# Weight splits spread over the slots behind the block ends of a merged stage, and shared between two engines around the projections

## The reference, cut to what matters

```python
h = rms_norm(x, norm_g); z = h @ w_in               # q, k, v, gates of both branches
# A: dilated window attention, 3 groups of 8 heads;  B: differential attention, 4 heads
ya = o_a * silu(ga);  yb = rms_norm(o_b, subln_g) * (1 - lam_init) * silu(gb)
pa = ya @ w_proj_a;   pb = yb @ w_proj_b
m = sigmoid(ma) * pa + sigmoid(mb) * pb
return x + m @ w_out                                # and the updated key/value caches
```

## Time and profile before

| | |
|---|---|
| median of 3 runs | 1908.26 us (1905.12 to 1911.16) |
| profiled execution | 1910.81 us, span 1908.8 us |
| mean granted TensorE clock | 0.938 |
| TensorE busy | 1681.4 us (88%) |
| VectorE, ScalarE, GpSimd busy | 707.4, 599.8, 680.1 us |
| chain that ended last, by engine | PE 76%, issue 6%, DMA 5%, POOL 5%, DVE 3%, ACT 2% |

### The profile page before, as it was taken

The page is one execution under the profiler, slowest core; times in us unless marked ns, Lnnn a source line. Parts: engine busy times, 40 slices in busy tenths (PEclk is TensorE's granted clock), DMA queues, the critical chain, the costliest instruction groups (busy, mean ns, idle before and its releaser), DMA issues.

```text
span 1908.8 us, 38064 instructions
## 1 busy us (share of the span) xinstructions
PE 1681.4 (88%) x14552; PEld 1371.5 (72%) x14552; DVE 707.4 (37%) x1751; ACT 599.8 (31%) x1393; POOL 680.1 (36%) x971
## 2 busy tenths in 40 slices
PE   4899698999899998999989779796879878789798
PEld 3677465788799998999977557574657646568587
DVE  4321266322272223622154433343344243358511
ACT  3321265422163222622152332333233233212200
POOL 3654311256443555345472310212121210266420
PEclk8999899999899998999989889798899988889899
DMA  4147400465515565265325757868678676655232
GB/s 150 45 153 266 156 24 21 159 214 186 186 42 197 208 219 186 58 229 193 106 77 186 256 189 241 265 230 283 210 265 259 230 264 230 199 172 195 92 120 83
DMA packets 164252, 336.24 MB, mean 176 GB/s; under 512 B 29873, under 2 KB 50738, under 8 KB 162674
## 3 DMA queue, kind: packets, MB, share of 16 engines
q1 hardware_dynamic: 142514, 212.86, 34.3%
q10 hardware_dynamic: 21568, 121.04, 18.0%
HBM read 294.05 MB, written 127.07 MB: 221 GB/s over the span
## 4 chain that ended last, share of the span: by engine, by line
PE 76%; issue 6%; DMA 5%; POOL 5%; DVE 3%; ACT 2%; SPq 2%; ACTq 0%; DVEq 0%; POOLq 0%
PE ps L1809 16%; PE ps L1810 15%; PE ps L1811 15%; PE ps L2004 4%; PE ps L1948 4%; DMA raw<-in_w_in 3%; PE ps L1899 3%; PE ps L1968 3%; PE ps L2046 3%; POOL w_lo L876 2%; PE ps L1955 2%; PE ps L1807 2%; PE ps L1808 2%; PE ps L2029 2%; PE ps L1920 1%
## 5 line engine op out<-in xcount | busy, mean ns | idle before, releaser
L1809 PE MATMUL ps<-w_hi,hT 128*128 128x512 f32 x1168 | 487.6, 417 | 27.9 <-issue 14.0
L1810 PE MATMUL ps<-w_lo,hT 128*128 128x512 f32 x1168 | 471.8, 404 | 0.0
L1811 PE MATMUL ps<-w_hi,hT 128*128 128x512 f32 x1168 | 471.6, 404 | 0.0
L876 POOL TENSOR_TENSOR w_lo<-raw,w_hi 128x512 fp32r<-128x512 f32 x145 | 185.6, 1288 | 436.0 <-ACT w_hi L1065 435.8
L1809 PEld LDWEIGHTS ps<-w_hi,hT 128*128 128x128 f32 x1168 | 275.1, 236 | 67.3 <-issue 18.3
L1811 PEld LDWEIGHTS ps<-w_hi,hT 128*128 128x128 f32 x1168 | 274.5, 235 | 37.6
L1810 PEld LDWEIGHTS ps<-w_lo,hT 128*128 128x128 f32 x1168 | 275.4, 236 | 33.2
L1546 DVE STREAM_TRANSPOSE k_in<-k_in 128x512 f32<-128x512 f32 x232 | 151.2, 689 | 129.2 <-DMA k_in<-in_cache_b_kv 69.8
L1065 ACT ACTIVATE w_hi<-raw 128x512 fp32r<-128x512 f32 x153 | 95.4, 630 | 266.5 <-DMA raw<-in_w_in 246.9
L969 POOL COPY q_rep<-qTs 32x96 f32<-32x96 f32 (+1 forms) x256 | 59.3, 232 | 212.9 <-issue 115.3
L856 POOL TENSOR_TENSOR rs<-ss,half_pow 128x8 f32<-128x8 f32 (+3 forms) x81 | 127.0, 1568 | 6.7
(11 more groups left out here) (217 smaller groups left out, 2583.7 us busy)
## 6 DMA issues: line engine op xcount, KB each, us to landing
out<-in_cache_a_kv ACTq DMA_DIRECT2D x32, 2040.0 KB, 9.3
k_in<-in_cache_b_kv SPq DMA_DIRECT2D x128, 256.0 KB, 4.0
v_in<-in_cache_b_kv SPq DMA_DIRECT2D x128, 256.0 KB, 4.8
raw<-in_w_in SPq DMA_DIRECT2D x104, 256.0 KB, 4.0
k_in<-in_cache_a_kv SPq DMA_DIRECT2D x104, 256.0 KB, 5.9
v_in<-in_cache_a_kv SPq DMA_DIRECT2D x104, 256.0 KB, 4.3
out<-in_cache_a_kv ACTq DMA_DIRECT2D x8, 2016.0 KB, 9.5
raw<-in_w_in ACTq DMA_DIRECT2D x40, 256.0 KB, 5.7
```

Of the source, the lines that this page charges most:

```text
L876: pool.tensor_tensor(lo, raw[:, q % 4, :], hi.bitcast(F32), ALU.subtract).then_inc(lo_done, 1)
L1809: pe.matmul(z, hi, wh, start=first, stop=False)
L1810: pe.matmul(z, hi, wl, start=False, stop=False)
L1811: return pe.matmul(z, lo, wh, start=False, stop=last)
```

## The change

Four things. (1) The gate table moves: the ninth tiles now stand in slots 6, 18, 30, 42 and 54, always with three slots without gates behind, and the last gates of the table in 58 to 68 in place of 56 to 66. (2) The seven splits at a block end leave `gate`: they stand two, two, two and one in the four slots behind the ninth tile, behind the copies of probabilities and the exponents; the spare chunk is split six slots behind the ninth tile; the raw loads stand behind the copies, one slot after the split of the chunk four before. (3) From chunk 153 to 167 the even chunks' w_lo is VectorE's. The first three splits of block b stand before `move_y(1, 0)`, the first three of the output block before `move_m(7)`. (4) `y_prepare` is cut in two, and tile 1's branch a part goes ahead of GpSimd's later splits; `turn_y(1, 0)` goes from before the last gate to behind `project(0, 0)`.

```diff
-GATE_SLOTS = (*range(7), *range(10, 19), *range(21, 30), *range(33, 42), *range(44, 53), 56, 58, 60, 62, 64, 66)
+GATE_SLOTS = (*range(7), *range(10, 19), *range(22, 31), *range(34, 43), *range(46, 55), 58, 60, 62, 64, 66, 68)
+BLOCK_ENDS = (6, 18, 30, 42, 54)
...
+        def by_vector(q):
+
+            return Q_PA <= q < Q_PB or (Q_PB < q < Q_OUT + KC and q % 2 == 0)
...
+        split_slot = {Q_GATE + KC: 2}
+        for block_, end_ in enumerate(BLOCK_ENDS):
+            q0 = Q_GATE + KC * (block_ + 1)
+            for k in range(1, KC):
+                split_slot[q0 + k] = end_ + (k + 1) // 2
+            if block_ < 4:
+                split_slot[q0 + KC] = end_ + 6
+        load_slot = {q + 4: at_ + 1 for q, at_ in split_slot.items() if q + 4 < Q_PA + 3}
...
         def prefetched(m):
 
-            if m == GATE_TILES - 3:
-                return range(Q_PB, Q_PB + SPARE)
...
+            return range(Q_PB, Q_PB + SPARE) if m == GATE_TILES - 3 else ()
...
+            splits_of(range(Q_PB + SPARE, Q_PB + 4))
+            y_prepare_a(1)
+            splits_of(range(Q_PB + 4, Q_OUT + SPARE))
...
+            def load_raw(q):
+                act.wait_ge(*lo_ready(q - 4))
+                act.dma_start(raw[:, q % 4, :], chunk_source(q)).then_inc(raw_in[q % 4], 16)
...
+                for q in loads_at(gg):
+                    load_raw(q)
...
+                for q in splits_at(gg):
+                    split_hi(*divmod(q, KC))
...
             store_gate(GATE_TILES - 1)
             move_y(0, 0)
+            for q in range(Q_PB + SPARE, Q_PB + 4):
+                split_hi(*divmod(q, KC))
             move_y(1, 0)
-            for q in range(Q_PB + SPARE, Q_OUT + SPARE):
+            for q in range(Q_PB + 4, Q_OUT + SPARE):
                 split_hi(*divmod(q, KC))
...
                 if i + 1 < TILES:
                     move_y(1, i + 1)
+                else:
+                    for q in range(Q_OUT + SPARE, Q_OUT + 4):
+                        split_hi(*divmod(q, KC))
                 if i:
                     move_m(i - 1)
...
             y_low(0, 0)
+            splits_of(range(Q_PB + SPARE, Q_PB + 4))
             y_low(1, 0)
+            splits_of(range(Q_PB + 4, Q_OUT + SPARE))
...
                     turn_y(0, 0)
-                    pe.wait_ge(s_oc, 2 * DEC_B)
-                    turn_y(1, 0)
                 gate(m)
...
                 project(0, i)
+                if i == 0:
+                    pe.wait_ge(s_oc, 2 * DEC_B)
+                    turn_y(1, 0)
```

More of the change, by code:

```diff
@@ L429, in weights @@
             return tuple((wx[:, n - 8] if n < RING else w2[:, n - RING])[:, part, :] for part in range(2))
+        def by_vector(q):
+            return Q_PA <= q < Q_PB or (Q_PB < q < Q_OUT + KC and q % 2 == 0)
         def lo_ready(q):
-            if Q_PA <= q < Q_PB:
-                return lo_pa, q - Q_PA + 1
-            return lo_done, q + 1 - (KC if q >= Q_PB else 0)
+            if by_vector(q):
+                return lo_pa, sum(by_vector(x) for x in range(Q_PA, q + 1))
+            return lo_done, q + 1 - sum(by_vector(x) for x in range(Q_PA, q + 1))
         def chunk_used(q):
@@ L1024, in _, with splits_of @@
                     if m == GATE_TILES - 2:
-                        y_prepare(0)
-            for q in range(Q_PB + SPARE, Q_OUT + SPARE):
-                split_lo(*divmod(q, KC))
+                        y_prepare_a(0)
+                        y_prepare_b(0)
+            def splits_of(chunks):
+                for q in chunks:
+                    if not by_vector(q):
+                        split_lo(*divmod(q, KC))
+            splits_of(range(Q_PB + SPARE, Q_PB + 4))
+            y_prepare_a(1)
+            splits_of(range(Q_PB + 4, Q_OUT + SPARE))
             for i in range(TILES):
                 if i + 1 < TILES:
-                    y_prepare(i + 1)
+                    if i:
+                        y_prepare_a(i + 1)
+                    y_prepare_b(i + 1)
                 if i:
                     merge(i - 1)
-            for q in range(Q_OUT + SPARE, Q_OUT + KC):
-                split_lo(*divmod(q, KC))
+            splits_of(range(Q_OUT + SPARE, Q_OUT + KC))
             merge(NT)
@@ L1065, in split_hi @@
                 act.activation(weights(q)[0], raw[:, q % 4, :], ACT.Copy).then_inc(hi_done, 1)
-                if Q_GATE + 5 <= q < Q_END - 3:
-                    act.wait_ge(*lo_ready(q - 1))
-                    act.dma_start(raw[:, (q + 3) % 4, :], chunk_source(q + 3)).then_inc(raw_in[(q + 3) % 4], 16)
+                if (Q_GATE + 5 <= q < Q_END - 3) and q + 3 not in load_slot:
+                    load_raw(q + 3)
             def input_step(i):
@@ L1724, in _ @@
                     y_low(1, i + 1)
+                else:
+                    splits_of(range(Q_OUT + SPARE, Q_OUT + 4))
                 if i:
                     m_low(i - 1)
+            splits_of(range(Q_OUT + 4, Q_OUT + KC))
             gated(1, NT)
```

20 lines of the change are left out of this document (11 added, 9 removed).

## The result

The changed kernel takes 1890.2 us (median of 8 runs, 1881.2 to 1895.2) where the kernel before takes 1906.8 (8 runs); the ratio is 0.9904, 95% interval 0.9881 to 0.9926. That is a cut of 18.3 us by the ratio (16.6 by the medians) where the forecast's sum was 36.9. The time lies in the range that was given (1849 to 1893), near its upper end, but outside the 25 to 50 us that the forecast itself claimed (chance 0.66): such a cut is the first rival's (6 to 25 us, 1895, chance 0.18).

What follows compares the result with a forecast made beforehand. TensorE bounds slots with gates; only block ends and the two seams around the projections can give. 25.4 + 7.5 + 4 = 36.9 us off 1910.8 gives 1873.9, against the median 1871 us; range 1849 to 1893.

Steps and rivals of the forecast that it cites:

- the first rival: Merged stage: slots without gates wait as long as before, only seams and first lines stay; cut 6 to 25 us, chance 0.18.
- The seams, 7.5 + 4: Around the projections, project(0, 0) starts 7.5 us earlier; before the output projection, splits moved ahead gain 4 us.
- The zyA wait: TensorE's 9.28 us wait for the next tile at the projections changes its cause, not its length; counted 0.
- VectorE and GpSimd in each other's way: Projection seam: shared splits may shut each other out; row says 1.0 us an operation; 0 to 3 us, outside the sum.
- What is late next at ends 6, 30, 54: Three block ends: b scores' chain, two splits and keys leave 8.4 us idle each instead of 15.6, 15.4 and 14.6.
- 7.2 + 7.0 + 6.2 + 1 + 2.5: Less idle time at slots 6, 30, 54 (first three terms); gains at the ends of slots 18 and 42 (last two).
- part one: Merged stage: splits spread over four slots, loads one slot later, a gate moved to the tail; gain 25.4 us.
- 2 us for the DMAs: Taken back at each of slots 6, 30, 54, as the same tiles must land in 7 us less.
- the clock at three ends: Slots 6, 30, 54: shorter waits keep TensorE's clock low for a shorter time; 1.5 us back at each.
- "Issue" at the score products stays: Block ends of slots 18 and 42: these waits stay, some 5 us in a usual slot n=3.
- The gain of 3 us at the tail: Slot 68 gets a gate from slot 56, which covers 3 of the tail's 4.2 us idle.
- The chains take it all back: Merged stage: slots without gates wait for keys, exponents and a split as long as before; time 1895, chance 0.18.

Runs made afterwards that it cites:

- e4: Changed kernel with VectorE's gated y of branch a for tile 1 put ahead of its low part of branch b and four splits; ratio 0.9912 to the kernel before.
- e1: Kernel before with only the new table of gate slots, splits still inside the ninth gate and both seams as before; 1904.6 us, ratio 0.9969.
- e2: Changed kernel's merged stage with the projections' and the output's seams of the kernel before; ratio 0.9945 to the kernel before.
- e7: Changed kernel with block ends moved to slots 8, 20, 32, 44, 56, last six gates moved, splits ahead of exponents and queries; 1886.4 us, ratio 0.9892.
- e5: Changed kernel with the merged stage's later key and value tiles loaded to half their width; 1858.4 us, ratio 0.9741 to the kernel before.
- e10: Changed kernel with tile 1's whole chains of branches a and b ahead of the second half of the projections' splits; ratio 0.9897 to the kernel before.

## Why the forecast's size was wrong and its sign right

- **The seams, 7.5 + 4: right.** The rest of the span fell by 11.4 us; the zyB wait went; the output projection's wait fell by 4.7. The zyA wait was forecast to change its cause and keep its length, and it is 9.28 us in both; e4 shows the cause named (splits on VectorE ahead of tile 1), and that removing a wait there saved at most a fifth of its length. That the length is the same to the hundredth is luck.
- **VectorE and GpSimd in each other's way: as small as the row said.** VectorE's timeline of the changed kernel has two operations of this seam drawn out beside one of GpSimd's (0.69 us else):
```profile
1651.33 1.35 DVE L1399 TENSOR_TENSOR w_lo<-raw,w_hi 128x512 fp32r<-128x512 f32 x1 [0.34 <-ACT w_hi L1097]
...
1666.45 1.80 DVE L1631 TENSOR_TENSOR ogA<-ogA 128x512 f32<-128x512 f32 x1
```
  That is 1.8 us of VectorE's time. The kernel before had two such operations here as well, 1.67 us in the earlier trace rows and 1.68 at 1666.98, together 2.0 us. The rule of the Trainium skill (SBUF — State Buffer, "Who interferes with whom") is seen in these rows, each of which runs until about 0.5 us after GpSimd's operation beside it, but sharing the splits added nothing to what was lost before.
- **What is late next at ends 6, 30, 54: right, 8.4 us each**; 7.4, 9.2 and 8.1 were measured. The 21.3 us taken from the copies' waits are near the size that was counted (7.2 + 7.0 + 6.2 + 1 + 2.5 = 23.9 us of idle time). But the fifth end gave less of it than was counted: in the kernel before, a gate in slot 56 stood right behind the exponent of slot 55, and the smaller copy cost 0.42 us beside the large one's 10.66,
```profile
1532.83 1.91 PE L2046 MATMUL ps<-v_in,pT 128*16 128x128 f32 x32 [10.66 <-ACT pT L1271]
```
  while now no gate stands behind that exponent and the smaller copy costs 8.12 (5.81 in e1, which has the new table alone).
- **The failed step is the size of part one, 25.4 us, which measured 6.6 in the stage (10.5 by e2's time).** It took the idle time removed from the copies as time gained, less "2 us for the DMAs" at three ends. What came back, by the table: 10.0 us at the values under "issue", 3.8 for value tiles, 3.4 for the last split's low part, 0.5 at the scores, less 1.2 elsewhere: 16.5, so idle time fell by 4.8 us, and TensorE's busy time by 1.7, where the forecast had 4.5 us for the clock at three ends. Of the 10.0, 4.8 us are ScalarE's queue: the raw loads were priced by their landing, but not by the wait that each carries past the copy behind it. Most of the other 5.2, and the 0.5 at the scores, are waits of another kind, TensorE's own instructions, of which the last section tells. With tiles of half or an eighth the value-tile term shrinks to 0.8 or 0.7 and ScalarE's stays.
- **"Issue" at the score products stays: right**, 41.3 and 41.8 us.
- **The gain of 3 us at the tail** can't be told from the table's other effects; e1 gives the table as a whole 5.9 us in time, of which its profile shows 1.4 in the stage and 2.5 in the rest.
- **The rivals.** "The chains take it all back" came nearest in time by a partly wrong mechanism: the chains took about the 8.4 us counted. Of the 16.5 us that came back 8.2 stood behind the moved loads and splits, 3.8 were value tiles, and about 4 TensorE's own instructions. That the time still lies in the range is owed to the range's width; the two terms of the seams are right, the one of the stage is not.

The "issue" at the values outside the two places above is 1.94 us inside a group of values at 1090, 2.59 at 1571, and waits of 0.4 us and less. Both large ones are of the kind in the last section. The one at 1571 is not even new: the kernel before has 3.43 us at the same count of products, where its table puts score products, and e1 has 2.45 at the values. What stays open is why these waits together grew by some 4 us.

## What to carry to other kernels

A moved step takes its waits along: price what stands behind it in each queue, a load's wait for its buffer too, and not only its own duration. A removed wait is worth its length less the next one in every chain that ended near it; move the two or three chains behind the same blocker together, or expect little (e4: 9.28 us removed, 1.7 gained in waits, nothing in the span). Measure by stretches that start at a common instruction: 4 us in the rest of the span were plain there and invisible in the median. And count instructions: a wait under "issue" that keeps its place in the count, whatever stands there, has another cause than the order of the work around it.

## What the runs showed of the hardware

**What the waits under "issue" inside a group are.** At the small score products they fall at the same places of TensorE's program in different kernels: inside a group, with the same number of products left behind. Before, changed, changed with half tiles, changed with an eighth:

```profile
1127.46 0.29 PE L2004 MATMUL ps<-k_in,q_rep 32*16 32x32 f32 x6 [3.96 <-issue]
```
```profile
1124.73 0.29 PE L2054 MATMUL ps<-k_in,q_rep 32*16 32x32 f32 x6 [3.96 <-issue]
```
```profile
1115.59 0.24 PE L2056 MATMUL ps<-k_in,q_rep 32*16 32x32 f32 x6 [2.04 <-issue]
```
```profile
1119.24 0.24 PE L2056 MATMUL ps<-k_in,q_rep 32*16 32x32 f32 x6 [2.04 <-issue]
```

Each of these has exactly 6174 products ahead of it, counted from the start of the program. In e7 the moved table puts other work at that count, the products with the new keys, and the wait stands there:

```profile
1118.02 0.29 PE L2064 MATMUL ps<-k_new,q_new 128*16 128x8 f32 x14 [4.67 <-issue]
```

So it belongs to a place in TensorE's list of instructions and not to what is done there. The places are evenly spaced. In the fourteen profiles 220 waits of the stage under "issue" are longer than 0.45 us. Of these 208 stand, to within 2 products, a multiple of 127.16 products behind the first (5156 products ahead of it); the other 12 are the two waits for s_oc in the six kernels that have them. The list of DMA queues on each kernel's page has a row of that spacing (packets, MB, share of the 16 engines):

```profile
q8 instruction: 115, 1.88, 0.4%
```

14552 products in 115 packets are 126.5 products a packet, with as many weight loads. The trace has the time of every packet: all 208 waits end 1.1 to 1.6 us after one of this queue has landed, while the 12 for s_oc end anywhere from 0.1 to 4.9 us after one. No semaphore is waited for inside such a group either. These waits are therefore for TensorE's own instructions, which come in portions over the DMA engines. 70 portions land in the stage, and TensorE waits at 13 to 18 of them.

The waits at the scores come to 39 to 50 us with whole tiles, 24 to 30 with half and 23 with an eighth: in the changed kernel some 18 us of it depend on the load of the DMA engines, and 23 do not. The e5 expectation had all of it going with the load. Their sizes at one place differ between kernels by up to 4 us (at 7191 products 5.1 before, 2.7 changed, 1.3 in e10), and no run here shows what sets them. No run took instructions away from TensorE either, which would tell what they cost in time.
